# Queries and keys made token by token on an unscaled input in the second block of a two-block transformer kernel

## The reference

```python
h = rms_norm(x, norm1_gain[l])
proj = jnp.einsum('bsd,dc->bsc', h, w_in[l])
q, k, v, lru_x, lru_g, gate_pre = jnp.split(proj, SPLIT_POINTS, axis=-1)
...
q = apply_rope_2(rms_norm(q, q_norm_gain[l]), cos, sin)
k = apply_rope_2(rms_norm(k, k_norm_gain[l]), cos, sin)
...
h2 = rms_norm(x, norm2_gain[l])
x = x + hierarchical_moe(h2, w_group_router[l], b_group_router[l],
                         w_expert_router[l], b_expert_router[l],
                         w_expert_gate[l], w_expert_up[l], w_expert_down[l])
```

## Time and profile before

| | |
|---|---|
| median of 3 runs (lowest to highest) | 1999.87 us (1998.81 to 2001.92) |
| the profiled execution, its own time | 2005.33 us |
| its span, first to last instruction | 2003.4 us |
| PE busy | 1861.3 us (93%) |
| DVE busy | 1187.6 us (59%) |
| ACT busy | 891.5 us (44%) |
| POOL busy | 353.4 us (18%) |
| mean granted PE clock | 0.967 of full speed |

### The profile page before, as it was taken

One profiled execution on the slowest core, in us unless ns is written; L12 is line 12 of the kernel. 1 busy time (PEld: TensorE's weight loads), 2 busy tenths in 40 slices (PEclk: granted clock), 3 DMA queues, 4 the chain that ended last, 5 costly groups with the idle time before them and its releaser, 6 DMA issues.

```text
span 2003.4 us, 26888 instructions
## 1 busy us (share of the span) xinstructions
PE 1861.3 (93%) x10912; PEld 1549.9 (77%) x10912; DVE 1187.6 (59%) x1628; ACT 891.5 (44%) x1425; POOL 353.4 (18%) x239
## 2 busy tenths in 40 slices
PE   6999999999999999997998888899999998999993
PEld 6988788999998788996776756765568876777772
DVE  5565534554474544554785476576753347788786
ACT  4425434333434434332431455347553235767672
POOL 3332221002423221003211065400000001000001
PEclk9999999999999999998998999899999978999997
DMA  5212102233222102242121101111243237999994
GB/s 172 69 62 71 43 22 79 70 104 95 75 66 67 59 22 85 64 132 73 64 74 53 64 22 42 43 64 63 84 158 105 85 133 280 374 384 380 376 374 175
DMA packets 155949, 241.61 MB, mean 121 GB/s; under 512 B 9313, under 2 KB 100738, under 8 KB 155826
## 3 DMA queue, kind: packets, MB, share of 16 engines
q1 hardware_dynamic: 148450, 213.07, 31.3%
q0 software_dynamic: 4464, 16.25, 2.1%
q10 hardware_dynamic: 2912, 10.55, 1.3%
HBM read 223.61 MB, written 16.25 MB: 120 GB/s over the span
## 4 chain that ended last, share of the span: by engine, by line
PE 80%; DVE 14%; ACT 2%; issue 2%; DMA 1%; POOL 1%; ACTq 0%; POOLq 0%; SPq 0%; DVEq 0%
PE acc L829 30%; PE acc L1061 16%; PE acc L1273 9%; PE acc L1046 4%; PE acc L928 4%; PE acc L992 3%; PE acc L1125 2%; DVE ring_split L2642 2%; PE acc L969 2%; DVE v L2393 1%; PE acc L1183 1%; PE acc L846 1%; DVE rt L2455 1%; PE acc L980 1%; DVE hres_split L2642 1%
## 5 line engine op out<-in xcount | busy, mean ns | idle before, releaser
L829 PE MATMUL acc<-h_split,ring_split 128*128 128x264 f32 x1088 | 309.8, 285 | 0.0
L829 PEld LDWEIGHTS acc<-h_split,ring_split 128*128 128x128 f32 x1088 | 205.8, 189 | 0.0
L1061 PE MATMUL acc<-h_split,ring_split 128*128 128x512 f32 x368 | 146.1, 397 | 0.0
L829 PE MATMUL acc<-h_split,qk_split 128*128 128x264 f32 x384 | 109.7, 286 | 0.0
L829 PE MATMUL acc<-ring_split,qk_split 128*128 128x264 f32 x384 | 108.7, 283 | 0.0
L2393 DVE RECIPROCAL v<-v 128x512 f32<-128x512 f32 x26 | 87.1, 3351 | 28.1 <-ACT v L1711 28.1
L829 PE MATMUL acc<-h_split,krope_split 128*128 128x264 f32 x320 | 94.7, 296 | 4.1 <-ACT latent L1611 2.6
L2058 DVE TENSOR_TENSOR ring_split<-ring,o_split 128x1024 fp32r<-128x1024 f32 (+1 forms) x32 | 45.1, 1414 | 80.6 <-ACT o_split L1432 80.6
L829 PE MATMUL acc<-ring_split,krope_split 128*128 128x264 f32 x320 | 91.5, 286 | 0.0
L2926 POOL DMA_INDIRECT latent<-h_rows,rows_of x16 | 18.1, 1132 | 397.2 <-PE acc L1259 229.9
L1273 PE MATMUL acc<-qk_split,krope_split 128*128 128x512 f32 x240 | 75.8, 397 | 8.6 <-DVE ring_split L2642 6.2
(11 more groups left out here) (557 smaller groups left out, 5767.0 us busy)
## 6 DMA issues: line engine op xcount, KB each, us to landing
ring<-in_w_in SPq DMA_DIRECT2D x64, 1024.0 KB, 5.3
ring<-in_w_expert_gate SPq DMA_DIRECT2D x13, 2048.0 KB, 9.7
ring<-in_w_expert_up SPq DMA_DIRECT2D x12, 2048.0 KB, 10.8
ring<-in_w_expert_down SPq DMA_DIRECT2D x11, 2048.0 KB, 11.4
ring<-in_w_out SPq DMA_DIRECT2D x12, 1024.0 KB, 5.2
hres<-in_w_expert_down SPq DMA_DIRECT2D x5, 2048.0 KB, 10.0
hres<-in_w_expert_up SPq DMA_DIRECT2D x4, 2048.0 KB, 11.0
y_rows<-gate ACTq DMA_DIRECT2D x16, 512.0 KB, 7.2
```

The source lines that it names most:

```text
L829: ins = nc.tensor.matmul(dst[0:rows_, half, 0:HALF], w[:, k, :], x[:, c], start=(k == 0 and i == 0), stop=(k == last and i == 2), skip_gro ...
L1061: ins = nc.tensor.matmul(dst[:, 0, :], w[:, k, :], x, start=(k == 0 and i == 0), stop=(k == DC - 1 and i == 2), skip_group_check=True)
```

## The change

- The input of the second block's projections is `xr` times the gain alone (`h2_up`, `h2_low`), split by ACT and DVE in the last products of the first block; the factor per token (`inv2` along the free axis, `scale_tok` per token tile) is applied to the results.
- q and k are made like the values, as 16 pairs (`wide_pair`, 48 products of 256 columns each), with the tokens on the partitions. Per pair ACT squares (128x512), DVE sums each of 8 sub-heads, ACT takes 2 small roots, DVE a reciprocal of 128x8, scales out of PSUM, multiplies by cosines and sines (tables with the gain in them) and adds, PE turns 4 blocks back (`pair_turn`), ACT copies out. The block and rotation products, the 128x512 reciprocals of this stage and POOL's part are gone. The input's factor cancels in the sub-head norm but for the epsilon (`eps_tok`).
- `inv2` multiplies `lx` and the 16 gate products on DVE on their way out of PSUM (`gate_in`; ACT's tanh is then in place), and `lg` on POOL, after the convolutions.
- The router works on the unscaled `h2`: 8 products with the router stationary and 512 tokens moving, seven of them laid between and behind the last `out2` products, 4 small turns to token rows, and the factor from squares that ACT sums out of the turned residual (`sq2`). The turned residual is copied out by DVE, but for its last tile.
- SP loads the rotary table and the gains during layer 1 instead of after the granule `q0`; four small loads at the start are gone.

The core of the diff:

```diff
-            def qk_sum(c):
-                product2(("qkss", c), act_evacuated, [blocks], on(tmp[c % 2]))
-            def qk_turn(c):
-                product2(("qkrot", c), dve_evacuated, [rot2], on(qk[:, c, 0:S]))
...
-            for c in range(1, 2 * DC + 2):
-                if 2 <= c < 2 * DC:
-                    product3(("qk", c), act_evacuated, h2_up, h2_low)
-                if 2 <= c <= 2 * DC:
-                    qk_sum(c - 1)
-                if c >= 2:
-                    qk_turn(c - 2)
+            def wide_pair(label, reader, name, i, pair, before=None):
...
+                dst = accumulator(label, reader)
+                w1, w0 = wide_up(i), weight2(name, ring_split)
+                for side in range(2):
+                    rows_ = slice((2 * pair + side) * P, (2 * pair + side + 1) * P)
                     for k in range(DC):
+                        if before and side == 0:
+                            before(k)
+                        for part, (x, w) in enumerate(((h2_up, w1[:, :, k, :]), (h2_low, w1[:, :, k, :]),
+                                                       (h2_up, w0[:, k, :]))):
+                            ins = nc.tensor.matmul(dst[:, side, 0:WIDE], x[k][:, rows_], w,
+                                                   start=(k == 0 and part == 0),
+                                                   stop=(k == DC - 1 and part == 2), skip_group_check=True)
+                done(ins, label)
...
+            def token_sums():
+                pe.wait_ge(square_sum, at(square_sum, "sum"))
+                dst = accumulator("ss_tok", dve_evacuated)
+                for i in range(QT):
+                    ins = nc.tensor.matmul(dst[:, 0, i:i + 1], sum_sq[:, META + i * P:META + (i + 1) * P], ones[:, 0:1],
+                                           start=True, stop=True)
+                done(ins, "ss_tok")
+                product2("ss_1", act_evacuated, [ones[:, :]], on(sum_sq[:, META:T]))
...
+            def pair_turn(u):
+                pe.wait_ge(dve_made, at(dve_made, ("tok2", u)))
+                dst = accumulator(("qkt", u), act_evacuated)
...
+                        ins = nc.tensor.transpose(dst[:, 0, c:c + P],
+                                                  tok2[u % 3][:, side * WIDE + head * P:side * WIDE + (head + 1) * P], ident)
+                done(ins, ("qkt", u))
+            for u in range(PAIRS):
+                g, pair = divmod(u, 2)
+                wide_pair(("qk", g, pair), dve_evacuated, f"{'qk'[g // 4]}{g % 4}", 2 * g, pair,
+                          (lambda k: pe.wait_ge(dve_made, at(dve_made, ("h2low", k)))) if u == 0 else None)
+                if u == 0:
+                    token_sums()
+                if u >= BEHIND:
+                    pair_turn(u - BEHIND)
...
+            def router_product(dst, k):
+                pe.wait_ge(dve_made, at(dve_made, ("h3", k)))
+                return nc.tensor.matmul(dst[0:GROUPS + EXPERTS, 0, :], router[:, k, :], h2[:, k, :], start=(k == 0),
+                                        stop=(k == DC - 1), skip_group_check=True)
+            def x_turn(i):
+                dst = accumulator(("x_tok", i), dve_evacuated if i < QT - 1 else act_evacuated)
...
+                for c in range(DC):
+                    ins = nc.tensor.transpose(dst[:, c * P:(c + 1) * P], xr[:, c, i * P:(i + 1) * P], ident)
+                done(ins, ("x_tok", i))
             for m in range(DC):
                 product3(("out2", m), dve_evacuated, m2_up, m2_low,
                          before=(lambda k: pe.wait_ge(dve_made, at(dve_made, ("m2low", k)))) if m == 0 else None)
-            product2("ss_2", act_evacuated, [ones[:, :]] * DC, lambda k: squares2[:, k, :],
-                     before=lambda k: pe.wait_ge(act_made, at(act_made, ("sq2", k))))
+                if m == DC - 3:
+                    to_logits = accumulator("logits", dve_evacuated)
+                    for k in range(DC - 3):
+                        router_product(to_logits, k)
+                elif m > DC - 3:
+                    router_product(to_logits, m - 1)
+            x_turn(0)
+            done(router_product(to_logits, DC - 1), "logits")
+            x_turn(1)
+            dst = accumulator("logits_tok", dve_evacuated)
+            pe.wait_ge(dve_evacuated, at(dve_evacuated, "logits"))
             for i in range(QT):
...
-            dst = accumulator("logits", dve_evacuated)
...
-                    ins = nc.tensor.matmul(dst[:, 0, 20 * i:20 * i + 20], h2[:, k, i * P:(i + 1) * P],
-                                           router[:, k, :], start=(k == 0), stop=(k == DC - 1))
-            done(ins, "logits")
...
+            done(ins, "logits_tok")
+            x_turn(2)
+            x_turn(3)
...
+                        nc.scalar.activation(h2_up[m], xr[:, m, :], ACT.Copy, scale=vec2[:, V_N1 + m:V_N1 + m + 1])\
...
-            root2("ss_1", tmp[2], D)
-            for c in range(DC):
-                act.wait_ge(dve_made, at(dve_made, ("h1", c)))
-                upper(h2_up[c], h2_full[c], ("h2up", c))
...
+            def pair_squares(u):
+                g, pair = divmod(u, 2)
+                act.wait_ge(psum_filled, at(psum_filled, ("qk", g, pair)))
...
+                made(nc.scalar.activation(tok2[u % 3].rearrange("p (a c) -> p a c", a=2), acc[:, slot, :, 0:WIDE], ACT.Square),
+                     ("squares2", u))
+            def pair_roots(u):
+                act.wait_ge(dve_made, at(dve_made, ("sums2", u) if u else "eps_tok"))
+                for side in range(2):
...
+                    ins = nc.scalar.activation(x, x, ACT.Sqrt, scale=1.0 / SUB, bias=eps_tok[:, i:i + 1])
+                made(ins, ("root2", u))
...
-                evacuated(nc.scalar.activation(gate[:, i % 2, 0:S], src, ACT.Tanh, scale=0.5,
...
+                act.wait_ge(dve_evacuated, at(dve_evacuated, label))
+                g = gate[:, i % 2, 0:S]
+                made(nc.scalar.activation(g, g, ACT.Tanh, scale=0.5, bias=half_bias[:, col:col + 1]), ("tanh2",) + label)
...
-                act.wait_ge(dve_evacuated, at(dve_evacuated, ("out2", m)))
-                made(nc.scalar.activation(squares2[:, m, :], xr[:, m, :], ACT.Square), ("sq2", m))
-            root2("ss_2", tmp[2], D)
...
+            def h2_lower(c):
+                dve.wait_ge(act_made, at(act_made, ("h2up", c)))
+                made(stt(out=h2_low[c], in0=xr[:, c, :], scalar=vec2[:, V_N1 + c:V_N1 + c + 1],
+                         in1=h2_up[c].bitcast(F32), op0=ALU.mult, op1=ALU.subtract), ("h2low", c))
...
-            inverse2("ss_1", 2)
-            for c in range(DC):
-                made(stt(out=h2_full[c], in0=xr[:, c, :], scalar=vec2[:, V_N1 + c:V_N1 + c + 1], in1=tmp[2],
-                         op0=ALU.mult, op1=ALU.mult), ("h1", c))
...
+            def pair_sums(u):
+                dve.wait_ge(act_made, at(act_made, ("squares2", u)))
+                made(nc.vector.tensor_reduce(norms[:, (u % 3) * HEADS:(u % 3 + 1) * HEADS],
+                                             tok2[u % 3].rearrange("p (h c) -> p h c", c=SUB), AX.X, ALU.add), ("sums2", u))
+            def pair_normed(u):
+                dve.wait_ge(act_made, at(act_made, ("root2", u)))
+                chain(nc.vector.reciprocal(x, x))
+                slot = n.slot(("qk", g, pair))
...
+                evacuated(tt(y, src, x.rearrange("p (a h) -> p a h", a=2).unsqueeze(3).to_broadcast([P, 2, 4, SUB]),
+                             ALU.mult), ("qk", g, pair))
...
+                tt(four(rope2_a), y, cos_[:, 2 * pair:2 * pair + 2, :].unsqueeze(2).to_broadcast([P, 2, 4, SUB]), ALU.mult)
+                for side in range(2):
+                    ins = tt(halves(four(rope2_b)[:, side]), turned_halves(y[:, side]),
+                             halves(sin_[:, 2 * pair + side, :].unsqueeze(1).to_broadcast([P, 4, SUB])), ALU.mult)
+                chain(ins)
+                made(tt(tok2[u % 3], rope2_a, rope2_b, ALU.add), ("tok2", u))
...
+                if u == 1:
...
+                    chain(nc.vector.reciprocal(inv2, inv2))
+                if u % 2:
+                    weights2_lower(u + 3)
+                    weights2_lower(u + 4)
...
+                for c in background2_at(s):
...
+                    evacuated(tt(lru_x[:, c, 1:1 + S], result2(("lx", c)), inv2, ALU.mult), ("lx", c))
...
+            def gate_in(label, i):
...
+                evacuated(tt(gate[:, i % 2, 0:S], result2(label), inv2, ALU.mult), label)
...
+                made(ts(h2[:, m, :], xr[:, m, :], vec2[:, V_N2 + m:V_N2 + m + 1], None, ALU.mult), ("h3", m))
                 weights2_lower(job_no2["out2", m] + 2)
-            inverse2("ss_2", 2)
-            for c in range(DC):
-                made(stt(out=h2[:, c, :], in0=xr[:, c, :], scalar=vec2[:, V_N2 + c:V_N2 + c + 1], in1=tmp[2],
-                         op0=ALU.mult, op1=ALU.mult), ("h3", c))
...
+            dve.wait_ge(act_made, at(act_made, "ss_2"))
```

(11 more changed lines are left out.)

290 lines of the change are left out of this document (149 added, 141 removed).

## The result

The changed kernel takes 1951.48 us (median of 4 runs, 1949.24 to 1954.95), the kernel before 2000.89 beside it (4 runs, 1998.81 to 2003.55). The ratio is 0.975, 95% interval 0.9732 to 0.9767: faster by 2.5%, 49.4 us. The forecast was 1940 with a range of 1932 to 1960. The profiled execution has a span of 1948.2 us, 55.2 less than before's, where the forecast's sum had 60.

The account below looks back on a forecast made before the run. PE, busy for 93% of the span, bounds most of the kernel, with serial chains at the stage's start and the router. Terms -47.0 + 1.0 - 14.0 = -60 us gave span 1943.4, median 1940, range 1932 to 1960.

Parts of the forecast that it names:

- Start and stage: From the last `out` product through queries, keys and values: 192.9 us becomes 145.4, net gain 47.0 us.
- with its cold clock: Start of the q and k stage: 30.0 us for what 14.56 would do, 15.4 us of the stage's gain.
- Rival 3: q and k stage paced by DVE's chain, hand-overs of 0.3 us, pair 7.0 us, 14 us more: 1954; chance 0.17.
- Rival 5: Pair products of the q and k stage run at 1.2 GHz, 73.5 us more: 2013, slower than before; chance 0.03.
- Added elsewhere: `lx` through DVE 0.3 us, gelu multiplications on POOL 0.2, gate products on DVE 0.5, mostly hidden: +1.0 in all.
- Rival 4: The gate multiplications on DVE are not hidden: 11 us, 1951; chance 0.06.
- Router: Last residual to bias addition 9.3 us; gain 12.2 there and 1.8 in the chain behind, 14 in all.
- The tail's clock: Turns at the router taken at 0.115 us each; at granted clock 0.50 they would cost 7.8 us more at most.
- Experts: From row numbers to the end: as long as before, unless loads set the pace and the earlier start is paid back.
- From span to median: Profiled execution before lay 5.5 us above the runs' median; the forecast span 1943.4 thus became a median of 1940.
- rival 1: Whole kernel paced as the forecast says: 1940, own range 1934 to 1950; chance 0.62.
- rivals 2: Router's gain swallowed by turns at 1.2 GHz (7.8 us) or loads pacing the experts (up to 12.2): 1950; chance 0.12.

Follow-up runs that it names:

- late_start: The changed kernel, but the first pair of q and k waits for the token sums and the token factor, as before the change: 1959.55 us.
- all_direct: The changed kernel without the token factor on lx, lg, ga and gl (doesn't compute the reference, for time alone): 1943.87 us, ratio 0.9693.
- split_first: The changed kernel with two lg low parts earlier in DVE's list and ACT's upper weight parts ahead of each gate's tanh: 1939.58 us, ratio 0.9679.

## Why the prediction was right, point by point

- **Start and stage.** Forecast -47.0, measured -46.84 (146.06 us against 145.4 plus 0.5). No gap, clock 1.00, pair 6.12 us. The one wait of PE for DVE behind the `inv2` reciprocal, at the fifth pair, was 0.59 (0.5 forecast). The name of the term at the start, "with its cold clock", misleads: of its 15.4 late_start gives back 10, only 2.0 of it clock, and in the kernel before DVE's multiplications, at 1.75 us beside POOL, held PE back as well. DVE's list was 5.47 us a pair for 5.4, but its busy time 80% (54.13 of 67.75), not 85 to 90. Rival 3 is refuted by the pair's pace: hand-overs within DVE's list are 0.03 us, not 0.3. Its pair of 7.0 would have taken 1.5 us more of DVE work, and DVE sets the pace from 0.65 on. Rival 5 did not occur: no window of the stage is under 1.00.
- **Added elsewhere.** Forecast +1.0, measured +3.8 by the table (9.42 less 5.6 for the router products), and 5.4 by all_direct. This is the step that failed. "Hidden, unless a gate's chain is the one PE waits for" was the right condition, judged by PE's full window in the rounds of `ga`; but the bill came at the window's end, where PE waits for the recurrence's last low part (1.95 us before, 3.81 after), a wait that the forecast hadn't looked up. By split_first this lateness is the order on ACT, whose upper parts stood behind the tanh, and not the 11 us of multiplications as such: with the order mended and DVE's work unchanged the wait is 1.95 again. About 2 of the 5.4 us are clock lost behind waits, a term that the forecast's sum for the middle didn't have. For `lx` and `lg` I put 0.3 and 0.2; PE's two waits grew by 1.12 and 1.37. Rival 4 (11 us) was right in kind, at about a third of the size at most.
- **Router.** Forecast 9.3 us behind the last residual, measured 9.40, but not through the terms as listed: a wait of 0.77 for PE at the turns of tile 1 was missing (its accumulator is the logits' own, four jobs earlier) and so was ACT's 0.19 per square for reading out the sum, while the hand-overs were shorter. The gain behind the bias was 0.7 (14.78 to 14.10), not 1.8. In all 18.84 less 5.6: 13.2 for 14.
- **The tail's clock.** Two windows of the changed kernel, in which nearly all products are turns, ran at a granted clock of 1.00 (the rows stand below the list); it fell only behind them, at 1593.3, in the stretch of small products. The rule of the Trainium skill, "TensorE: Matmul & The Clock Gate", Part 4: PE-mode transpose, is not borne out here: the clock stayed where the full products ahead had put it. Whether turns alone would raise it from 0.50 no run shows.
- **Experts.** 348.40 for 348.44: moved as a whole, in spite of a DMA share of 1.02.
- **From span to median.** A span 55.2 us shorter in place of 60 explains 4.8 of the 11.5 us between 1940 and 1951.5. The other 6.7 are the reference: the profiled execution of before lay 5.5 us above its median, the one of after 1.3 below its own. The forecast carried the 5.5 over unchanged. Over all comparisons the kernel before ran from 1996.6 to 2008.1. So the mechanism was right and the number partly fortunate: 1951.5 lies just above rival 1's own range (1934 to 1950), beside the times of rivals 2 and 4, neither of which came about in full, and inside the range because that was held open for rival 3.

```profile
1581.00:1584.00 3.00, 2.79 (x25) 2.51 (x25) 1.65 (x3) 2.62 (x5) 0.00 (x0) 1.00 0.94 363
1584.00:1588.00 4.00, 3.15 (x29) 2.91 (x28) 3.65 (x10) 3.10 (x5) 0.00 (x0) 1.00 0.03 10
```
